# Five edits at the seams between stages of a two-block transformer kernel on one Trainium2 core

## The reference

```python
h = h + HALF_STEP * swiglu_ffn(rms_norm_2(h, ffn1_norm[layer]), w_gate, w_up, w_down)   # D_FF 2816
h = h + conformer_conv(rms_norm_2(h, mix_norm[0]), ...)   # layer 0
#   a, gate = split(u @ w_pw1 + b_pw1);  c = a * sigmoid(gate)
#   c = depthwise causal convolution of c with 31 taps + b_dw
#   c = silu(layer_norm(c));  c @ w_pw2 + b_pw2
h = h + stick_breaking_attention(...) @ w_o               # layer 1
def rms_norm_2(x, g):
    y = x * rsqrt(mean(x * x, axis=-1) + 1e-6)
    return y * g
```

## Time and profile before

| what | value |
|---|---|
| median of 3 runs | 2513.57 us |
| the profiled execution | 2511.76 us, span 2510.0 us |
| TensorE, VectorE, GpSimd, ScalarE busy | 99%, 41%, 39%, 29% |
| granted TensorE clock | 0.995 of full speed |
| HBM traffic | 91 GB/s over the span |

### The profile page before, as it was taken

The page is one execution under the profiler, slowest core; times in us unless marked ns, Lnnn a source line. Parts: engine busy times, 40 slices in busy tenths (PEclk is TensorE's granted clock), DMA queues, the critical chain, the costliest instruction groups (busy, mean ns, idle before and its releaser), DMA issues.

```text
span 2510.0 us, 30052 instructions
## 1 busy us (share of the span) xinstructions
PE 2483.5 (99%) x11638; PEld 1981.9 (79%) x11638; DVE 1027.2 (41%) x1489; ACT 735.6 (29%) x963; POOL 974.5 (39%) x305
## 2 busy tenths in 40 slices
PE   9999999999999999999999999999999999999998
PEld 7777887777888888568888888888888767888887
DVE  6363615458222317974223110422321686522301
ACT  3454225523222222242222222222122453222221
POOL 3322243204444442124444444444444663444442
PEclk9999999999999999999999999999999999999999
DMA  4222132212222233512222233322223211222232
GB/s 161 100 84 84 67 118 76 93 51 84 100 100 90 85 110 103 154 36 99 100 100 80 92 113 121 131 100 100 85 92 126 83 35 51 101 100 86 84 103 79
DMA packets 42752, 235.81 MB, mean 94 GB/s; under 512 B 5552, under 2 KB 5552, under 8 KB 22448
## 3 DMA queue, kind: packets, MB, share of 16 engines
q1 hardware_dynamic: 41808, 231.55, 26.9%
q10 hardware_dynamic: 864, 3.15, 0.3%
HBM read 222.86 MB, written 6.29 MB: 91 GB/s over the span
## 4 chain that ended last, share of the span: by engine, by line
PE 70%; DVE 3%; issue 3%; POOL 1%; ACT 1%; SPq 0%; DMA 0%; DVEq 0%; ACTq 0%; POOLq 0%
PE ps L1679 22%; PE ps L1680 22%; PE ps L1681 22%; PE ps L2069 1%; PE ps L2180 1%; PE ps L2160 1%; PE ps L2197 1%; PE ps L2186 1%; POOL w_lo L579 1%; DVE w_lo L1142 0%; DVE conv_out L1508 0%; SPq L543 0%; DVE tmp L1508 0%; PE ps L2170 0%; DVE tmp L1613 0%
## 5 line engine op out<-in xcount | busy, mean ns | idle before, releaser
L579 POOL TENSOR_TENSOR w_lo<-raw,w_hi 128x2048 fp32r<-128x2048 f32 (+1 forms) x204 | 863.7, 4234 | 1365.1 <-ACT w_hi L709 1342.7
L1679 PE MATMUL ps<-x_hi,w_hi 128*128 128x512 f32 x2047 | 809.3, 395 | 2.0 <-POOL w_lo L579 1.4
L1681 PE MATMUL ps<-x_hi,w_lo 128*128 128x512 f32 x2047 | 797.8, 390 | 0.0
L1680 PE MATMUL ps<-x_lo,w_hi 128*128 128x512 f32 x2047 | 797.5, 390 | 0.0
L1679 PEld LDWEIGHTS ps<-x_hi,w_hi 128*128 128x128 f32 x2047 | 384.6, 188 | 101.4 <-issue 20.8
L709 ACT ACTIVATE w_hi<-raw 128x2048 fp32r<-128x2048 f32 (+1 forms) x215 | 375.7, 1748 | 286.3 <-PE ps L1681 281.5
L1681 PEld LDWEIGHTS ps<-x_hi,w_lo 128*128 128x128 f32 x2047 | 384.5, 188 | 81.0
L1680 PEld LDWEIGHTS ps<-x_lo,w_hi 128*128 128x128 f32 x2047 | 384.9, 188 | 77.2 <-issue 0.7
L1189 DVE TENSOR_TENSOR tmp<-ps,rms_b 128x512 f32<-128x512 f32 x88 | 60.9, 691 | 585.4 <-PE ps L1681 582.4
L1681 PE MATMUL ps<-hid_hi,w_lo 128*128 128x512 f32 x704 | 273.9, 389 | 0.0
L1679 PE MATMUL ps<-hid_hi,w_hi 128*128 128x512 f32 x704 | 273.9, 389 | 0.0
(11 more groups left out here) (255 smaller groups left out, 2436.4 us busy)
## 6 DMA issues: line engine op xcount, KB each, us to landing
raw<-in_w_up SPq DMA_DIRECT2D x88, 1024.0 KB, 4.8
raw<-in_w_down SPq DMA_DIRECT2D x64, 704.0 KB, 4.0
raw<-in_w_feat SPq DMA_DIRECT2D x22, 1024.0 KB, 4.8
raw<-in_w_pw SPq DMA_DIRECT2D x12, 1024.0 KB, 5.1
raw<-in_w_tok SPq DMA_DIRECT2D x8, 1024.0 KB, 4.9
raw<-in_w_out SPq DMA_DIRECT2D x8, 1024.0 KB, 4.8
shifted<-conv_in SPq DMA_DIRECT2D x80, 67.5 KB, 2.0
bias<-in_bias_t SPq DMA_DIRECT2D x8, 512.0 KB, 5.9
```

Source lines behind the costliest of these rows:

```text
L579: nc.gpsimd.tensor_tensor(w_lo[:, s, 0:w], raw[:, s, 0:w], w_hi[:, s, 0:w].bitcast(f32), ALU.subtract).then_inc(lo_ready, 1)
L1679: nc.tensor.matmul(out, hi, src_hi, start=start, stop=False, skip_group_check=True)
L1680: nc.tensor.matmul(out, hi, src_lo, start=False, stop=False, skip_group_check=True)
L1681: return nc.tensor.matmul(out, lo, src_hi, start=False, stop=stop, skip_group_check=True)
```

## The change

- ScalarE rounds chunk 3 of out0 and out1 behind the squares of chunk 0, ahead of those of chunk 1 (`third_ahead`).
- SyncE issues 8 of the 16 shifted copies of m = 1; ScalarE issues the other 8 behind the gate of tile 6, ahead of the rounding of pw2's chunk 0.
- `add_squares` is a scalar_tensor_tensor with a factor 1.0 instead of a tensor_tensor; so it is in every stage but the layer norm.
- The gain of final_gain is a scalar_tensor_tensor with a column of zeros, broadcast, as the second input, instead of a tensor_scalar.
- The eight products of x with `gain_rms` follow two by two behind the hidden pairs 1 to 4 of up0, as scalar_tensor_tensors.
- The rows of final_gain stand after k = 7 of up0's first chunk instead of k = 6.

```diff
@@ -538,7 +538,7 @@
             sp.wait_ge(conv_gated, m + 1)
             if m >= SHIFT_RING:
                 sp.wait_ge(conv_done, m - SHIFT_RING + 1)
-            for shift in range(SHIFTS):
+            for shift in range(SHIFTS // 2 if m == 1 else SHIFTS):
                 for b in range(SHIFTS):
                     sp.dma_start(shifted[CB * shift:CB * (shift + 1), m % SHIFT_RING, b, :],
                                  conv_in[CB * b:CB * (b + 1), j, shift:shift + SHIFTED]).then_inc(shifts_made[m], 16)
@@ -731,14 +731,14 @@
             act.wait_ge(rms_row_done, turn_no[name] + 1)
             nc.scalar.activation(rms_b[:, :], ps[:, 7, :], ACT.Copy).then_inc(rms_ready, 1)
 
-        def layer(name, finish, norm=False, second_rounded=False):
+        def layer(name, finish, norm=False, second_rounded=False, third_ahead=False):
 
             at = phase_names.index(name)
             following = phase_names[at + 1] if at + 1 < len(phase_names) else None
             pairs = phase_chunks[name] // 2
 
             def pair(i, last=False, first_pair=False):
-                if not (first_pair and second_rounded):
+                if not (first_pair and second_rounded or third_ahead and not first_pair):
                     high_part(name, i, 1)
                 rounded_ahead = first_pair and name in ("att_in0", "up0")
                 if rounded_ahead:
@@ -755,6 +755,8 @@
                     high_part(following, 0, 0)
                 if first_pair:
                     finish(i, 0)
+                if first_pair and third_ahead:
+                    high_part(name, 1, 1)
                 finish(i, 1)
 
             pair(0, last=pairs == 1, first_pair=True)
@@ -925,7 +927,7 @@
                     act.wait_ge(ret_sums, h0 + s + 1)
                     nc.scalar.activation(ret_root[:, ST * s:ST * (s + 1)], ps[:, 4 + s, 0:ST],
                                          ACT.Sqrt, scale=1.0 / RET_DIM, bias=eps_rms).then_inc(ret_roots, 1)
-            layer(f"out{l}", squares_of_two(["att_in1", "final_gain"][l]), second_rounded=True)
+            layer(f"out{l}", squares_of_two(["att_in1", "final_gain"][l]), second_rounded=True, third_ahead=True)
             if l == DEPTH - 1:
                 high_part("up0", 0, 1)
                 root_of("final_gain")
@@ -951,6 +953,13 @@
             if isinstance(i, int) and i == KD // 2 - 1 and s:
                 conv_move(0)
             gate(i, s)
+            if isinstance(i, int) and i == KD // 2 - 1 and not s:
+                act.wait_ge(conv_gated, 2)
+                for shift in range(SHIFTS // 2, SHIFTS):
+                    for b in range(SHIFTS):
+                        act.dma_start(shifted[CB * shift:CB * (shift + 1), 1, b, :],
+                                      conv_in[CB * b:CB * (b + 1), CONV_ON_PE[1], shift:shift + SHIFTED])\
+                            .then_inc(shifts_made[1], 16)
 
         layer("pw1", pw1_finish, norm=True)
         high_part("pw2", 0, 1)
@@ -1072,8 +1081,8 @@
 
             dve.wait_ge(squares_ready, KD * norm_no[norm] + j + 1)
             dve.wait_ge(squares_summed, KD * sum_no[norm] + j)
-            nc.vector.tensor_tensor(sq_sum[:, :], sq_sum[:, :], tmp[:, slot, :], ALU.add)\
-                .then_inc(squares_summed, 1)
+            nc.vector.scalar_tensor_tensor(out=sq_sum[:, :], in0=sq_sum[:, :], scalar=1.0, in1=tmp[:, slot, :],
+                                           op0=ALU.mult, op1=ALU.add).then_inc(squares_summed, 1)
 
         def clear_sum(norm):
             n = sum_no[norm]
@@ -1164,8 +1173,9 @@
                     dve.wait_ge(x_updated, updates[norm] + j + 1)
                     if gain:
                         add_squares(norm, j, 4 + t)
-                        nc.vector.tensor_scalar(x[:, j, :], x[:, j, :], col(gain, j), None, ALU.mult)\
-                            .then_inc(x_gained, 1)
+                        nc.vector.scalar_tensor_tensor(out=x[:, j, :], in0=x[:, j, :], scalar=col(gain, j),
+                                                       in1=zeros[:, 0:1].to_broadcast([P, SEQ]), op0=ALU.mult,
+                                                       op1=ALU.add).then_inc(x_gained, 1)
                         dve.wait_ge(x_gained, j + 1)
                     split(j, split_gain, x_split)
                     if not gain:
@@ -1199,10 +1209,13 @@
 
             if n == 0:
                 up_pair(0)
-                for j in range(KD):
-                    ins = nc.vector.tensor_tensor(x[:, j, :], x[:, j, :], gain_rms, ALU.mult)
+                for i in range(1, KD // 2 + 1):
+                    up_pair(i)
+                    for j in (2 * i - 2, 2 * i - 1):
+                        ins = nc.vector.scalar_tensor_tensor(out=x[:, j, :], in0=x[:, j, :], scalar=1.0, in1=gain_rms,
+                                                             op0=ALU.mult, op1=ALU.mult)
                 then(ins)
-            pairs_of(up, up_pair, per=4, start=1 if n == 0 else 0)
+            pairs_of(up, up_pair, per=4, start=KD // 2 + 1 if n == 0 else 0)
 
             clear_sum(next_norm)
             if split_no.get(next_split):
@@ -1774,7 +1787,7 @@
 
             fitted = [{}, {}]
             if norm == "up0":
-                fitted = [{3: lambda: norm_sums("final_gain"), 6: lambda: norm_rows("final_gain")},
+                fitted = [{3: lambda: norm_sums("final_gain"), 7: lambda: norm_rows("final_gain")},
                           {4: sums, 5: rows}]
             elif norm in in_rows:
                 fitted = [{KD - 2: sums}, {}]
```

## The result

The changed kernel took **2522.28 us** (median of 8 runs, 2518.47 to 2524.83) against 2513.32 (8 runs, 2511.68 to 2515.82) for the one before: a ratio of **1.0035, interval 1.0026 to 1.0043**, 9.0 us slower. The forecast was 2520.4, with 2512.6 to 2522.8 as its range; the median lies 0.5 us under the upper end. The profiled execution took 2521.96 with a span of 2520.2, against 2511.76 and 2510.0.

What follows compares the result with a forecast made beforehand. TensorE, busy 99% of the span, was taken as the bound, leaving only its idle pieces to gain. The terms -0.6 + 5.1 (out1's seam) - 1.1 + 3.4 gave +6.8 us, 2520.4 (chance 0.50), range 2512.6 to 2522.8.

Steps and rivals of the forecast that it cites:

- The lock: VectorE and GpSimd: an operation arriving while GpSimd holds the port ends 0.56 us after it (0.27 for tensor_scalar), two-input form included.
- Square sums at 0: Square sums as scalar_tensor_tensor: same inputs, same lock, same 0.69 us each, so 0 by itself.
- Gain at +0.27 each: Gain of final_gain as scalar_tensor_tensor with zeros: +0.27 us on VectorE, 8 times, its cost lying in the order of arrival.
- T+3.83 against T+4.02: Out1's seam, from update start T: GpSimd arrives at T+3.83, second square sum at T+4.02 (before T+3.76), so GpSimd is ahead.
- Out0 -0.6: Last chunk of out0: with chunk 3 rounded ahead, TensorE's wait goes, -0.6 us.
- out1 -1.8 given back +1.8: Out1: chunk 3 rounded ahead saves 1.8 us, then up0's first chunk gives it back entirely, +1.8.
- sums +6.0: Up0's first chunk: TensorE waits from 585.0 to 591.05 for the last square sum before final_gain's sums, +6.0 us.
- rows -0.9: Rows of final_gain, moved behind k = 7 in up0's first chunk, find their reciprocal ready: -0.9 us.
- fifth chunk -1.1: Up0's fifth chunk: dealing the row products to pairs removes TensorE's wait, -1.1 us.
- The shifted copies at +3.4: Convolution: eight issues on ScalarE delay rounding, VectorE's remainder and taps, so TensorE waits before the mean, +3.4 us.
- rival 1: Out1's seam: the last square sum slips ahead of GpSimd, seam costs 0.8, total +2.5 us, 2516.1; chance 0.17.
- rival 2: Convolution: ScalarE issues the shifted copies at no cost, so nothing is lost there, total 2517.0 us; chance 0.10.

Runs made afterwards that it cites:

- e4: The kernel before with only the square sums changed, to scalar_tensor_tensor: 2512.98 us (10 runs), ratio 0.9995 (0.9986 to 1.0004).

## Why the prediction was right, and where it was not

The likeliest case is what happened, and the time came 1.9 us above it, within the range; the change itself was +9.0 where +6.8 was forecast. Point by point:

- **The lock** held in every form that was asked of it. The Trainium skill, "SBUF — State Buffer", section "Who interferes with whom", says that the order of issue decides who blocks. The trace of this seam agrees to a fifth of a microsecond: 0.19 behind GpSimd a square sum takes 4.98, 0.08 ahead of it 0.69. In the convolution two traces of six go against it (last section).
- **Square sums at 0**: right (e4's 0.69 and 5.10).
- **Gain at +0.27 each, and its effect on the order**: right, to the hundredth. T+3.83 against T+4.02 was worked out from two intervals of the trace before and stands so in the trace after. The experiment with the gain back gives all of it, wait and clock: 8.4 us.
- **Out0 -0.6, out1 -1.8 given back +1.8, sums +6.0, rows -0.9, fifth chunk -1.1**: measured -0.56, -1.78, +2.05, +5.79, -1.15, -1.27.
- **The shifted copies at +3.4**: the mechanism was right, the term too large; it is 2.2 (2.18 in the trace after, 2.08 alone). The step that failed is "TensorE wants them for the mean at 1066.91 and had 0.45 to spare": the row at 1066.91 reads `tmp` and not `conv_out`. VectorE's delay was 3.6 (3.9 forecast). The copies for m = 4, expected 1.1 late, made nobody wait.
- **TensorE's clock** is the term that was missing. The prediction gave a wait its length and 0.16 us for the restart. Behind the 5.54 us wait there are 2.7 us more, behind the 2.18 us wait 1.5. The forecast's sum with the shifts at 2.2 and both stretches is 6.8 - 1.2 + 4.2 = +9.8, against 9.0 measured in the medians. That the medians give less may be because the clock does not fall behind every short wait (behind the one before the mean it fell in two of the four traces that have it); this is argued, not shown.
- **Rivals.** In none of the three traces with the long gain did the square sum slip ahead of GpSimd (rival 1), though elsewhere an operation of VectorE did (last section), and the issues are not free (rival 2).

That the sum came within 1.9 us is partly luck: a term 1.2 too large stood against two that were left out, 4.2 together.

## What to carry to other kernels

Where two engines share a lock and their starts lie 0.1 or 0.2 us apart, every operation ahead of them that changes its length can change the order, and what matters is who waits for the loser: here 0.27 us on a gain that TensorE did not wait for cost 8.4. Work out both arrivals from a common start before lengthening anything, and when a seam is sped up, look at what the freed engine will ask for next (1.8 us gained at out1, 2.05 lost at up0). A wait of TensorE is priced with what its clock can lose behind it, and its slack is read from the instruction that reads the late tile, not from the first of its line.

## What the runs showed that was not expected

- Behind a wait of 5.54 us (two traces of two) TensorE's products lie 0.427 us apart instead of 0.227 for about 4 us, and eight small ones take 1.87 instead of 0.94: half as much again on top of the wait. Waits of 1.9 to 2.2 us had it in some executions and not in others: before the mean in two of four (the 16 taps in 3.44 and 3.29, against 1.93 and 1.92), before up0 in one of three.
- Being ahead is not always enough to get the port. VectorE's remainder of pw2's chunk 0 took 3.38 us before and 2.29 in the run with the square sums' form alone, and in both GpSimd's add had started 0.46 to 0.47 ahead of it, while VectorE's operation before it was still running. The add of the kernel before, then add and remainder of that run:

```profile
1034.16 1.69 POOL L638 TENSOR_TENSOR tmp<-conv_out 128x512 f32<-128x512 f32 x1 [71.74 <-ACT conv_out L947]
...
1035.65 3.90 POOL L638 TENSOR_TENSOR tmp<-conv_out 128x512 f32<-128x512 f32 x1 [71.65 <-ACT conv_out L947]
...
1036.12 2.29 DVE L1142 TENSOR_TENSOR w_lo<-raw,w_hi 128x2048 fp32r<-128x2048 f32 x1
```

Six traces have these two so placed: in four GpSimd won and the remainder was stretched, in two (this one and the dealt row products) GpSimd stood until the remainder ended. In the row products of up0 GpSimd lay 0.01 or 0.02 ahead 28 times in ten traces, and VectorE kept the port 27 times. The square sums behind an `x_lo` had GpSimd 0.19 to 0.50 ahead of them 110 times in ten traces, and GpSimd won every time. What decides is not shown. With the copies on ScalarE the remainder comes ahead of the add and takes 2.29, but the operation behind it then takes 1.51 instead of 0.47, so nothing of the delay is paid back.

- Eight small copies cost ScalarE's queue 0.65 us each, as on SyncE's queue, against 0.54 for the larger input tiles, and ScalarE starts nothing in between.
